# A hybrid retention and latent-attention layer on one core: the order of the next head's projection units inside the attention steps

## The reference, cut to what matters

```
k_nope, v = mla_decompress(ckv, w_ukv)          # keys and values of 8 heads from a 256-wide latent
s = (einsum(q_nope, k_nope) + einsum(q_rope, kpe)) * scale
p = softmax(where(mask, s, min))                # a 64-row chunk sees itself and all earlier ones
out = einsum(p, v)
```

## Time and profile before

| | before |
|---|---|
| median of three runs | 2007.88 us (2007.42 to 2008.55) |
| the profiled execution | 2008.58 us, its span 2006.8 us |
| PE busy | 1955.7 us, 97% |
| DVE, ACT, POOL busy | 1373.7, 832.6, 405.9 us |
| mean granted clock of TensorE | 0.993 |
| odd heads 3 and 5, from one `pt_hi` memset of POOL to the next | 49.5 us each |
| even heads 2 and 4, the same | 42.1 us each |

### The profile page before, as it was taken

How to read it: one execution, slowest core, us unless ns; L and a number is a source line. 1 busy time by engine, 2 the same in 40 slices (tenths; PEclk the granted TensorE clock), 3 DMA queues, 4 the chain that set the end, 5 groups by cost and what they waited for, 6 DMA issues and landing times.

```text
span 2006.8 us, 35964 instructions
## 1 busy us (share of the span) xinstructions
PE 1955.7 (97%) x14476; PEld 1891.3 (94%) x14476; DVE 1373.7 (68%) x2152; ACT 832.6 (41%) x1426; POOL 405.9 (20%) x350
## 2 busy tenths in 40 slices
PE   8989999999999998999999999999999999999998
PEld 8978888888989998999999989999999999999998
DVE  6567776766567556877678996866656656586676
ACT  5334444442223235555553434643333333333343
POOL 0110000001245432000000000154544444300012
PEclk9999999999999999999999999999999999999999
DMA  8211010133255546767757553122322323484322
GB/s 321 100 40 33 25 33 22 33 141 135 74 176 185 171 168 234 257 203 235 246 197 249 210 181 138 67 97 88 114 82 93 114 82 107 148 315 155 130 84 90
DMA packets 114452, 279.63 MB, mean 139 GB/s; under 512 B 13424, under 2 KB 29744, under 8 KB 107760
## 3 DMA queue, kind: packets, MB, share of 16 engines
q1 hardware_dynamic: 114288, 277.34, 39.5%
HBM read 192.13 MB, written 85.16 MB: 138 GB/s over the span
## 4 chain that ended last, share of the span: by engine, by line
PE 83%; DVE 11%; issue 2%; ACT 2%; DMA 1%; POOL 0%; SPq 0%; DVEq 0%; ACTq 0%; POOLq 0%
PE ps L1272 25%; PE ps L1273 25%; PE ps L1274 25%; DVE s_lo L2364 1%; DVE t_lo L2364 1%; PE ps L1465 1%; DVE tmp L2371 1%; DVE negmax L2593 1%; PE ps L1367 1%; PE ps L1373 1%; PE ps L1584 1%; DVE pt_lo L2364 1%; PE ps L1565 1%; PE ps L1561 1%; PE ps L1562 1%
## 5 line engine op out<-in xcount | busy, mean ns | idle before, releaser
L1272 PE MATMUL ps<-s_hi,t_hi 128*128 128x272 f32 x1344 | 390.8, 291 | 10.7 <-DVE s_lo L2364 9.8
L1273 PE MATMUL ps<-s_hi,t_lo 128*128 128x272 f32 x1344 | 389.2, 290 | 0.0
L1274 PE MATMUL ps<-s_lo,t_hi 128*128 128x272 f32 x1344 | 387.9, 289 | 0.0
L1272 PE MATMUL ps<-sx_hi,t_hi 128*128 128x272 f32 x1232 | 355.9, 289 | 0.6 <-issue 0.6
L1273 PE MATMUL ps<-sx_hi,t_lo 128*128 128x272 f32 x1232 | 356.1, 289 | 0.0
L1272 PEld LDWEIGHTS ps<-s_hi,t_hi 128*128 128x128 f32 x1344 | 255.3, 190 | 12.5 <-DVE s_lo L2364 8.8
L1273 PEld LDWEIGHTS ps<-s_hi,t_lo 128*128 128x128 f32 x1344 | 255.0, 190 | 0.0
L1274 PEld LDWEIGHTS ps<-s_lo,t_hi 128*128 128x128 f32 x1344 | 255.0, 190 | 0.0
L1274 PE MATMUL ps<-sx_lo,t_hi 128*128 128x272 f32 x880 | 254.7, 289 | 0.0
L1272 PEld LDWEIGHTS ps<-sx_hi,t_hi 128*128 128x128 f32 x1232 | 234.0, 190 | 0.7 <-issue 0.6
L1273 PEld LDWEIGHTS ps<-sx_hi,t_lo 128*128 128x128 f32 x1232 | 233.5, 190 | 0.0
(11 more groups left out here) (291 smaller groups left out, 4795.8 us busy)
## 6 DMA issues: line engine op xcount, KB each, us to landing
t_row<-in_weights SPq DMA_DIRECT2D x48, 512.0 KB, 5.5
s_raw<-s_x SPq DMA_DIRECT2D x21, 1088.0 KB, 6.2
w_stage<-in_weights SPq DMA_DIRECT2D x35, 512.0 KB, 3.8
piece<-gate_spill SPq DMA_DIRECT2D x44, 272.0 KB, 5.6
s_y<-hg SPq DMA_DIRECT2D x44, 272.0 KB, 2.1
d_raw<-s_y SPq DMA_DIRECT2D x7, 1632.0 KB, 8.0
raw<-in_weights SPq DMA_DIRECT2D x22, 512.0 KB, 4.6
hg<-in_weights SPq DMA_DIRECT2D x22, 512.0 KB, 4.4
```

What stands on the lines that cost most here:

```text
L1272: nc.tensor.matmul(out, wh, xh, start=start, stop=False, skip_group_check=onto)
L1273: nc.tensor.matmul(out, wl, xh, start=False, stop=False, skip_group_check=onto)
L1274: return nc.tensor.matmul(out, wh, xl, start=False, stop=stop, skip_group_check=onto)
```

## The change

In odd heads K1 comes before R0; they are the two fill units of step 2, so only their order in the step changes. In even heads from 2 on the list of units is the same (K, Q, V), but they lie in other steps. Head 0 and head 7 keep theirs.

```diff
     elif head % 2:
-        fill = [("M", head + 1, *unit) for unit in (("K", 0), ("Q", 0), ("R", 0), ("K", 1), ("R", 1), ("Q", 1), ("Q", 2),
+        fill = [("M", head + 1, *unit) for unit in (("K", 0), ("Q", 0), ("K", 1), ("R", 0), ("R", 1), ("Q", 1), ("Q", 2),
                                                     ("R", 2), ("K", 2), ("V", 0), ("V", 1), ("V", 2))]
         counts = (2, 0, 2, 2, 1, 2, 0, 2, 1)
     else:
         fill = [("M", head + 1, kind, g) for kind in "KQV" for g in range(NG)]
-        counts = (0, 2, 0, 2, 0, 2, 0, 2, 1) if head else (0, 1, 0, 2, 0, 2, 0, 1, 1)
+        counts = (1, 1, 1, 2, 0, 2, 0, 2, 0) if head else (0, 1, 0, 2, 0, 2, 0, 1, 1)
```

## The result

The changed kernel takes 2013.31 us (median of 12 runs, 2011.58 to 2015.73), the kernel before, run beside it, 2008.97 us (2006.73 to 2010.84). The ratio is **1.0021, 95% interval 1.0013 to 1.0028**: slower by 4.3 us, 2.6 to 5.6 by the interval. The forecast was +3.0, within a range of -2.9 to +5.6. The time itself, 2013.31 us, lies just inside the range of 2005 to 2013.5, since the kernel before stood 1.1 us higher beside it than in its first three runs. The sign and the main term are right. Two terms are off in size, and they partly cancel.

The account below looks back on a forecast made before the run. PE is 97% busy, but odd heads were taken as bound by DVE's chain from R0's rotation, even heads by the last `pt_lo`. +4.0 + 0.3 - 1.3 = +3.0 us against 2007.88 gave 2010.9 us, range 2005 to 2013.5.

Parts of the forecast that it names:

- the main term: Odd heads 1, 3, 5: K1 ahead of R0 delays DVE's chain, +4.0 us in all.
- Odd heads: R0's rotation on DVE starts 2.01 us later, shrinking to 1.34 at `qr`; T of tile 6 late, 1.34 per head.
- In-order queue: DVE takes its list strictly in order, so the rotation waits behind `k_lo`; odd heads cost 4.0 us, otherwise 1.0.
- Even heads, the term: Even heads with K0, K1, K2 in steps 0, 1, 2: +0.1 us each, +0.3 in all.
- PE does Q0 and Q1 (3.84): Even heads, step 3: this pair replaces K2 and Q0 (3.60 us), making T of tile 3 0.8 late.
- K2 hurts more: Rival, even heads: DVE's full 1.0 us delay reaches each head's end, +3.0 there, +5.7 in all, 2013.6 us; chance 0.13.
- Reload: Head 6's earlier Q2 triggers the reload 1.25 us sooner against PE, gaining -1.3 us in the first retention unit.
- The bound of 2.6 us: Reload's largest possible gain: all of PE's waits for the last three tiles in the first retention unit.
- The rival by which PE's waits are the cost: Rival, odd and even heads: DVE keeps up and PE's covered waits are won, -9.4 us, 1998.5 us; chance 0.12.
- even heads gain: Rival: PE's lead carries over in even heads while odd heads lose, -1.2 us, 2006.7 us; chance 0.12.
- The reload isn't sooner: Rival, head 6: V1 or V2's triggers or the store before them hold the queue, +4.3 us, 2012.2 us; chance 0.13.
- No `issue` wait of PE: Sign in odd heads: PE would show none of its waits for a bank to be read.

Follow-up runs that it names:

- run 1: Only the odd heads' order changed (K1 ahead of R0) against the kernel before, even heads as before; 2014.27 us, ratio 1.0024.
- run 3: Against the kernel before: odd heads' K1 ahead of R0, with ACT copying K1's high part before tile 3's exponential; 2010.92 us, ratio 1.0006.
- Run 9: Against the kernel before: even-head K0, K1, K2 in steps 0, 1, 2, V2 in step 8; odd-head Q2 copy before tile 5's exponential; 2007.36 us, ratio 0.9990.
- run 2: Only the even heads' steps changed, as in the change, against the kernel before, odd heads as before; 2010.61 us, ratio 1.0006.
- run 8: Against the kernel before: odd-head R0 moved to step 1, K1 in step 2 with its ACT copy before tile 3's exponential; 2011.42 us, ratio 1.0013.
- run 11: Against the kernel before: ACT copies Q2 (odd heads) and K2 (even heads) before the exponential; even-head K0, K1, K2 in steps 0, 1, 2, V2 in step 8; ratio 0.9973.

## Why the prediction was right, and where its sizes were off

**Odd heads, right to a tenth.** In the time of before: O at 280.74 (predicted 280.7), `k_lo` 280.02 (280.0), the rotation 280.56 to 283.38 (280.56 to 283.37), `qr` 285.60 (285.58), Q2 290.79 (290.7), R2 297.46 (297.4), T of tile 6 304.96 (304.95). Each head lost 1.36 to 1.40 where 1.34 stood in the sum; three heads 4.2, against 4.0. Runs 1 and 3 show the cause by undoing it: with the copy ahead, 0.8 of 1.4 is gone. Run 9 shows from the other side that this stretch goes by DVE: a shorter pause there moves the head although PE's wait of 1.41 stays where it is.

**In-order queue.** DVE stood idle for 1.37 us before `k_lo`, and for the last part of it R0 was ready: in run 3, where nothing but PE held it, the rotation began at 279.74 in the time of before, and in the change `k_lo` began at 280.02. DVE didn't take the rotation in these 0.28 us. This agrees with the strict order that the Trainium skill gives for this queue ("TensorE: Matmul & The Clock Gate", section "Architectural detail"). No run changes the order on DVE alone, so nothing more than this shows it.

**Even heads, the term was mis-sized: +0.1 each predicted, +0.54, +0.40 and +0.37 measured** (+0.50 to +0.53 in run 2). The steps up to T of tile 2 hold (235.17 against 235.2), and Q0 begins at 238.63 (238.6). The failed step is "PE does Q0 and Q1 (3.84)". That row was of Q1 with Q2, and Q2 has 320 columns where Q0 and Q1 have 384. The right row was that of R1 with Q1. Here is first the window of Q0 with Q1 after, then that of R1 with Q1 before:

```profile
240.82:245.10 4.28, 4.28 (x24) 4.24 (x25) 2.66 (x6) 1.36 (x3) 0.00 (x0) 1.00 0.09 31
```

```profile
284.00:288.17 4.17, 4.17 (x27) 4.13 (x25) 3.81 (x8) 1.18 (x3) 0.00 (x0) 1.00 0.09 31
```

So T of tile 3 came 1.28 late (242.91 against 241.63) instead of 0.8, and Q1's low part with it. DVE then was a full microsecond late at tile 7's maximum, not 0.5, and this is the case that I had as the rival "K2 hurts more", though 0.4 to 0.5 of that microsecond reach the end of the head, 1.3 us in all where the rival had 3.0. The end of the head is as predicted: V1's and V2's low parts, P of tile 8, then `pt_lo`, and PE waits 0.83 for it.

```profile
265.00 1.21 DVE L2364 TENSOR_TENSOR v_lo<-ps,v_hi 128x512 fp32r<-128x512 f32 x3 [1.26 <-ACT v_hi L1852]
266.13 0.14 DVE L2600 RECIPROCAL rowsum<-rowsum 64x1 f32<-64x1 f32 x1
266.31 0.38 DVE L2601 TENSOR_SCALAR p_exp<-p_exp,rowsum 64x320 f32<-64x320 f32 x1
266.61 1.27 DVE L2364 TENSOR_TENSOR pt_lo<-ps,pt_hi 128x512 fp32r<-128x512 f32 x2
```

**Reload.** From head 7's mark to the end of the first retention unit 13.59 us (458.24 to 471.83) against 15.20 (451.99 to 467.19): -1.6, predicted -1.3. The instruction behind the unit, in the kernel before and in the changed one, and the one wait for a tile that is left in the unit after:

```profile
467.19 0.60 PE L1465 MATMUL ps<-eye,p_exp 128*128 128x128 f32 x4
```

```profile
468.59 0.44 PE L1272 MATMUL ps<-xn_hi,w_hi 128*128 128x384 f32 x1 [0.35 <-DMA xn_lo<-xn_spill]
...
471.83 0.38 PE L1465 MATMUL ps<-eye,p_exp 128*128 128x128 f32 x2
```

The first trigger came 17.8 us ahead of the mark instead of 16.5, so 1.3 sooner, as forecast, but this is in part luck. Within head 6 it came 1.0 sooner (25.05 us behind the head's mark, before 26.02), since PE was later there than the 0.85 of the prediction; the rest is that the head ended 0.4 later, the very loss that the even heads' term had missed. The remaining 0.3 of the gain lies within what the five kernels with the change's even steps differ by among themselves (13.5 to 14.2). The bound of 2.6 us for PE's waits in this unit was too high: by start times its 24 matmuls, one each 0.17 to 0.18 us, leave about 2.2 of the 6.4 us up to 467.19, and 0.6 of them are left after.

**The sum.** 4.2 + 1.3 - 1.6 = 3.9 us by the heads, 4.3 by the medians, 3.0 forecast. By the chances given, the outcome of 0.21% slower lies on the border between "within 0.2%" (0.60) and "slower" (0.28). The rival by which PE's waits are the cost is refuted, as is "even heads gain". "The reload isn't sooner" would have given nearly the measured time for a wrong reason: the reload was sooner, and the even heads took the gain.

**The signs.** `k_lo` with 1.4 us idle before it, `qr` 1.3 later and K2's pause came as announced. Three signs did not. "No `issue` wait of PE" in odd heads contradicts the prediction's own working, which had PE wait for the banks of K1, R1 and Q2; the three waits of 0.67 to 0.70 fit the working. PE's wait before T of tile 6 is not larger (1.04 against 1.06), as PE itself comes later to it. And an even head is not at 42.2 but at 42.5 to 42.6.

## What to carry to other kernels

When an engine that waits is not the one that sets the time, follow the chain to the instruction that releases it, and ask whether the edit starts that chain later; here an order that took away half of PE's longest wait started DVE's chain 2 us late. In a pair such as ACT's copy and DVE's subtraction the order on each engine can differ from PE's: the copy belongs ahead of an exponential that is not ready yet, and two such swaps on ACT alone took the slower order from 1.0021 back to 1.0000 of the time before. Before a row stands in for another unit, compare their shapes.

## What the runs showed of the hardware

**VectorE's normalising waits until a GpSimd operation beside it is done.** The normalising of tile 3 (128x512) took 1.15 us in head 3 after, and 0.61 before. Neither is its time alone: where POOL does nothing beside it, it takes 0.48 or 0.49 in all 13 profiles. In the kernel before, in head 2 without POOL and in head 3 beside it:

```profile
237.65 0.49 DVE L2601 TENSOR_SCALAR p_exp<-p_exp,rowsum 128x512 f32<-128x512 f32 x1
```

```profile
282.12 0.61 DVE L2601 TENSOR_SCALAR p_exp<-p_exp,rowsum 128x512 f32<-128x512 f32 x1
```

After, it began at 286.33, just behind POOL's addition:

```profile
286.19 1.02 POOL L3192 TENSOR_TENSOR tmp<-tmp,tmp 128x384 f32<-128x384 f32 x1 [14.08 <-DVE tmp L2371]
```

It began 0.14 us into the addition after and 0.68 before, and yet it ended at the same distance behind it, 0.27 and 0.28. In all 36 such cases of the profiles it is 0.27 to 0.29; with 128x640 it is 0.34 to 0.36 in 39 cases (0.75 instead of 0.55), with 128x384 in run 8 it is 0.22 (1.06 instead of 0.42). So the operation ends a fixed time behind POOL's, whether it began early or late in it. Nothing is lost where POOL is nearly done: 128x896, begun 0.68 or 0.69 into an addition of 0.87 to 0.89, took its own 0.69. The Trainium skill ("SBUF — State Buffer", section "SBUF: two separate sides") describes a port pair that a GpSimd operation and a VectorE operation in a two-port mode take as an exclusive lock for a whole instruction, whichever starts first. No view names the mode, but all these cases fit it. In the change it cost nothing, as `qr` waited 0.26 for ACT behind it anyway; in run 8 PE waited for it.

It goes the other way round too. At the start of an even head POOL has two memsets of 0.53 us, and DVE normalises tile 0 (128x128, 0.29 alone). In 29 of 39 heads DVE took 0.70 to 0.74 and ended 0.07 to 0.09 behind the second memset; in the other 10 it took 0.28 or 0.29, and the second memset 0.60 to 0.62. Where K0 stands in step 1, such a head is 0.3 us shorter (head 6 of run 1, head 4 of run 8), since PE waits there for tile 0. Heads 4 and 6 of the changed kernel are of this kind and head 2 is not, which may be why they lost 0.1 less; in run 2 none is, and the three lost 0.50 to 0.53.

**The granted clock fell in head 0, and not in every execution.** In the stretch from 140 to 145 us the granted clock was 0.68 in the profile of the change and 1.00 in that of before:

```profile
140.00:145.00 5.00, 4.64 (x12) 2.33 (x11) 2.03 (x7) 1.58 (x4) 0.00 (x0) 0.68 0.03 7
```

From 140 to 143 us it was 0.50, which is 1.2 and not 2.4 GHz, and the key unit there took 2.98 us by start times (140.01 to 143.00) instead of 1.50. PE had waited several times just before, in both kernels (2.6 us while the units V0 to V2 of head 0 ran, 1.2 before K0 of head 1, 0.7 before T of tile 0), so these waits alone don't decide it. Head 0 is the same in all kernels. In four of the 13 profiles (before, runs 1, 8 and 11) the clock was 1.00 in this stretch, and the head took 50.7 us from mark to mark; in the other nine it was 0.66 to 0.80, and the head took 51.9 to 52.4. Between the two spans here, 4.9 us apart, it makes 1.5 us, of which a different start took 0.7 back; this is why the heads, not the spans, were compared.
